# Each weight piece of a 128-partition ring brought by two transfers of 64 partitions

## The reference

```python
h = h + _token_mixer(h, ...)                       # w_in, w_out
xs = jax.vmap(lambda ub, ib: ub[ib])(u, idx)       # 34 tokens' worth of slots an expert (cap = 2 * 272 // 16)
hid = silu(einsum('becd,edf->becf', xs, w_gate)) * einsum('becd,edf->becf', xs, w_up)
y = einsum('becf,efd->becd', hid, w_down) * g      # 16 experts: 1024 x 2816, 1024 x 2816, 2816 x 1024
```

## Time and profile before

| | us |
|---|---|
| median of 3 runs (3094.57 to 3104.59) | 3099.58 |
| the profiled execution, its own time | 3092.36 |
| its span | 3090.6 |
| PE busy in the span | 2585.5 (84%) |
| DVE busy | 900.4 (29%) |
| ACT busy | 411.6 (13%) |

### The profile page before, as it was taken

One profiled execution on the slowest core, in us unless ns is written; L12 is line 12 of the kernel. 1 busy time (PEld: TensorE's weight loads), 2 busy tenths in 40 slices (PEclk: granted clock), 3 DMA queues, 4 the chain that ended last, 5 costly groups with the idle time before them and its releaser, 6 DMA issues. The chain is left out here.

```text
span 3090.6 us, 43919 instructions
## 1 busy us (share of the span) xinstructions
PE 2585.5 (84%) x19739; PEld 1398.1 (45%) x19739; DVE 900.4 (29%) x1834; ACT 411.6 (13%) x811; POOL 85.4 (3%) x93
## 2 busy tenths in 40 slices
PE   7969568999999998889999899865666877869995
PEld 4525234334333343434433344343665876645553
DVE  0227543102212122221312031135448532143222
ACT  1032001100100001111211121011113221010001
POOL 0010000000000000000000000000000100000000
PEclk9988668899999999999999999986788988979998
DMA  5317037898999988988898979951010012159997
GB/s 183 109 41 268 33 127 291 339 390 333 388 380 371 364 359 354 403 345 342 336 396 354 371 295 368 378 189 61 1 35 1 3 57 99 68 224 419 422 422 293
DMA packets 158868, 789.17 MB, mean 255 GB/s; under 512 B 18241, under 2 KB 20553, under 8 KB 110937
## 3 DMA queue, kind: packets, MB, share of 16 engines
q1 hardware_dynamic: 155225, 773.78, 63.1%
q0 software_dynamic: 3456, 12.58, 1.0%
HBM read 774.79 MB, written 11.53 MB: 254 GB/s over the span
## 5 line engine op out<-in xcount | busy, mean ns | idle before, releaser
L2975 PE MATMUL bank<-ring,arena 128*34 128x512 f32 (+1 forms) x3072 | 700.0, 599 | 76.1 <-DMA ring<-in_w_up 61.9
L2975 PEld LDWEIGHTS bank<-ring,arena 128*34 128x34 f32 x3072 | 177.7, 117 | 490.5 <-issue 467.1
L2999 PE MATMUL bank<-ring,arena 128*34 128x512 f32 x1408 | 321.6, 600 | 46.2 <-DMA ring<-in_w_down 45.4
L2999 PEld LDWEIGHTS bank<-ring,arena 128*34 128x34 f32 x1408 | 80.0, 112 | 278.0 <-issue 152.3
L303 PE MATMUL bank<-arena,ring 128*128 128x256 f32 (+1 forms) x688 | 158.7, 394 | 11.8 <-DMA ring<-in_w_in 9.7
L303 PEld LDWEIGHTS bank<-arena,ring 128*128 128x128 f32 x688 | 134.0, 195 | 36.7 <-issue 10.5
L3439 PE MATMUL bank<-ring,arena 128*64 128x256 f32 x992 | 111.1, 379 | 3.2 <-DMA ring<-in_moe_w_up 2.4
L2875 PEld LDWEIGHTS bank<-arena 64*64 64x64 f32 x2304 | 76.8, 141 | 53.0 <-issue 52.6
L313 PE MATMUL bank<-ring,arena 128*128 128x512 f32 (+1 forms) x224 | 98.8, 596 | 0.0
L3439 PEld LDWEIGHTS bank<-ring,arena 128*64 128x64 f32 x992 | 72.7, 137 | 45.2 <-issue 12.5
L2987 PEld LDWEIGHTS bank<-consts,arena 34*128 34x128 f32 x704 | 82.4, 191 | 14.9 <-issue 14.1
(11 more groups left out here) (630 smaller groups left out, 3018.1 us busy)
## 6 DMA issues: line engine op xcount, KB each, us to landing
ring<-in_w_gate SPq DMA_DIRECT2D x128, 1408.0 KB, 9.2
ring<-in_w_up SPq DMA_DIRECT2D x128, 1408.0 KB, 12.3
ring<-in_w_down SPq DMA_DIRECT2D x176, 1024.0 KB, 8.5
ring<-in_w_in SPq DMA_DIRECT2D x46, 1024.0 KB, 6.7
ring<-in_moe_w_down SPq DMA_DIRECT2D x33, 1024.0 KB, 14.9
ring<-in_moe_w_gate SPq DMA_DIRECT2D x31, 1024.0 KB, 13.6
ring<-in_moe_w_up SPq DMA_DIRECT2D x31, 1024.0 KB, 16.5
ring<-in_ada_w SPq DMA_DIRECT2D x24, 1024.0 KB, 7.0
```

The lines of the kernel that those rows point to most:

```text
L2975: last = mm(ps[c][row:row + CAP, 0:n], xsT[:, e, k, :], w[:, at:at + n], start=k == 0, stop=k == KT - 1)
L2999: last = mm(ps[6][row:row + CAP, :], hidT[:, 2 * j + f, :], w[:, f, half * BANK:(half + 1) * BANK], start=j + f == 0, stop=j == FT // 2 - ...
```

## The change

Every piece is now two transfers: rows 0 to 63 of the slot, then rows 64 to 127. Both add 16 to the same semaphore, so what PE waits for becomes 32 a piece. SP's wait for `piece_used` stands ahead of the first of the two. The 32 experts' own loads at the end stay one transfer of 128 partitions; only the value from which they count on is now the doubled one. Nothing else is touched: PE, DVE, ACT and POOL have the same instructions in the same order.

```diff
@@ -165,8 +165,8 @@ piece
-            pieces.append((src, view, k, 16 * slot_count[k]))
-            return view, landed[k], 16 * slot_count[k], n
+            pieces.append((src, view, k, 32 * slot_count[k]))
+            return view, landed[k], 32 * slot_count[k], n
@@ -752,7 +752,7 @@
-        tile_count0 = [16 * n for n in slot_count] + [0] * (len(moe_slots) - RING)
+        tile_count0 = [32 * n for n in slot_count] + [0] * (len(moe_slots) - RING)
@@ -813,7 +813,8 @@ issue
                     if n >= RING:
                         sp.wait_ge(piece_used, n - RING + 1)
-                    sp.dma_start(view, src).then_inc(landed[k], 16)
+                    for rows in (slice(0, P // 2), slice(P // 2, P)):
+                        sp.dma_start(view[rows], src[rows]).then_inc(landed[k], 16)
```

## The result

The changed kernel takes 4051.26 us, median of 4 runs (4044.80 to 4076.47), against 3102.09 us of the kernel before (3094.57 to 3104.88): 1.307 times as long, 95% interval 1.304 to 1.310, or 949 us more. The profiled execution has a span of 4043.0 us, 952.4 more than before. The forecast was 4210 us, 3250 to 4400.

The account below looks back on a forecast made before the run. It took DMA and PE as nearly even in the experts' stretch, with little DMA rate to spare. 3092.4 (profiled execution) + 1104 + 10 = 4206, which lies 7.2 us under the runs' median, so 4210 us; range 3250 to 4400.

Parts of the forecast that it names:

- What bounds the kernel: In the experts' stretch, 470 to 2070 us, DMA and PE are nearly even, with a tenth of the DMA's rate spare.
- Issues on SP: About 437 more transfers among the experts, 0.33 to 0.37 us an issue, hidden behind earlier pieces: cost nothing.
- a second completion: Where PE waits for a DMA, a second completion a piece costs 16 us at most, taken as 5.
- The rate of 64 partitions: Ring pieces in halves take twice as long, less 0.1 us a half: gate or up 6.58 us, 1 MB 4.94.
- The sum: Experts' stretch: DMA time grows by 1254 us, 150 us absorbed by idle time, so the stretch grows by 1104 us.
- Outside the experts: Where phases start with an empty ring, first pieces come 2.4 us later each: none to 20 us, taken as 10.
- PE's clock: Among the experts, PE busy about 53%, its granted clock below 0.94; at 0.61 a step stays covered, at 0.5 100 us more.
- The rate is kept: Rival for the ring's transfers: 16 engines carry halves at the whole's rate, 3099.6 + 5, up to 3116 us; chance 0.17.
- The engines fall out of step: Rival for the ring's queue: both halves written at once, half the loss, 3620 us, 3250 to 4050; chance 0.14.
- A little faster: Rival in the down product: two shorter transfers cover each other's ends, 18 us gained, 3082 us; chance 0.03.

Follow-up runs that it names:

- The streams: Programs without computation that only load w_gate pieces into six slots, by lists of partition ranges: whole 427 GB/s, halves 217, partitions 0 to 15 alone 108.
- the stream of 96 pieces: No computation, only w_gate pieces loaded in halves, lower then upper, 96 pieces without a break: 218 GB/s over 580 us without a rise.

## Why the prediction was right, step by step

*What bounds the kernel.* The middle stretch with DMA and PE nearly even was the right place: 925 of the 952 us lie there.

*Issues on SP, and a second completion, at nothing and 5 us.* An issue took 0.55 to 0.61 us, not the 0.33 to 0.37 that I had taken over from whole pieces. Right as far as a tiny second issue and a completion go (0.2 us, inside the interval). But cutting a piece costs 20 us even where both cuts go at full rate. That is 15 us more than my term, and it was above the 16 us that I had set as its most. The 5 us don't stand in the sum that gave 4206, either.

*The rate of 64 partitions.* The step on which all rests held: factor 2, less a little. It rested on one weak row, the 16 partitions at 175 GB/s. The streams confirm the mechanism and correct that row: 16 partitions in a steady stream get 108, so one transfer of 64 KB at the start of the program read too high. A gate or up piece took 6.62 us (forecast 6.58), one of 1 MB 4.69 (4.94).

*The sum.* The stretch grew by 925 us, not 1104. The DMA's time, share times length, went from 0.89 x 1549 = 1379 us to 1.00 x 2476 = 2476: by 1097, where I had 1254. The 0.89 is read from the kernel before:

```profile
471.00:2021.00 1550.00, 1412.80 (x10168) 601.02 (x10168) 312.03 (x604) 183.43 (x384) 27.01 (x16) 0.95 0.89 359
```

Three terms were off. The mean rate was 225 GB/s, mine 562.9 MB / 2598 us = 216.7, so the 557.1 MB of the stretch took 95 us less (about half of it the 1 MB pieces, if all came in 4.69 us; the rest is the stretch at 259 GB/s and the 226 to 235 behind it). I had counted 562.9 MB, 5.8 too many: eight `w_in` pieces are issued behind the last `w_down`, and some small loads were left out: 27 us. And I took 1343 us for the DMA's time before, and it was 1379: 36 us. Absorbed idle time was 1549 - 1379 = 170 us against 150. All of this pulls the same way, some 179 us, and what lies outside the experts pulls 17 us the other way: 4206 would have become 4044, the time of the profiled execution. The 4051 us of the result lie at the very edge of the 4050 to 4400 that I had given for this mechanism: the mechanism was right, and the size that I gave it too large by about a sixth (1114 us against 949).

*Outside the experts* 27 us against 10. 20 of them are ahead of the experts, 12.8 us of these in waits for `ada_w` that weren't there before. I hadn't looked at that loop; the remaining 7 us ahead were not traced. With halves for `w_gate` and `w_up` alone the experts start only 4 us late, with halves for the others 19 us, so it is the other pieces that cost them.

*PE's clock* fell to 0.81, not as far as the 0.61 with which I had bounded it. PE's busy time in the stretch rose with it from 1413 to 1687 us for as many matmuls, so it was not 53% of the stretch but 68%; it stayed covered by the DMA, as forecast.

*The rivals.* "The rate is kept" is refuted by the change and by partitions 0 to 63 alone (206). "The engines fall out of step" would fit the 255 us at 259 GB/s and their end when the queue runs dry, but my ground for it, that they would drift apart in a queue that never runs dry, fell with the stream of 96 pieces; what happens in those 255 us is open. "A little faster" fell with the columns and the even and odd partitions: two transfers at full rate were 20 us slower than one, not faster.

## What to carry to other kernels

What counts in a transfer to SBUF is how evenly its partitions are spread over the ways into it, not only how many they are: 0 to 63 got 206 GB/s, 32 to 95 got 425, even and then odd partitions 426, every eighth 215. If a load has to come in two parts, cut along the free axis or into even and odd partitions (0.7% here) and not at partition 64 (31%). And a DMA share of 1.00 with 217 GB/s under it is a queue that is held up: read the share and the rate together.

## What the runs showed of the hardware that I had not expected

- Transfers to different partitions hardly make up for each other in one queue: eight transfers of 16 partitions gave 130 GB/s where one of them alone gave 108, halves gave 217 where one half alone gave 206, and a small transfer ahead of them left the halves at 216 to 218.
- Lower halves from SP's queue and upper halves from ACT's, under way together, gave 244 GB/s, 12% above the 217 of one queue.
- An issue on SP of 64 partitions takes longer than one of 128: 608 against 368 ns for `w_down`.
- In both profiles of the changed kernel the halves ran at about 260 GB/s in the same 250 us of the program, in the first at up to 327 GB/s right before the queue ran dry, and at 213 to 235 elsewhere.
